# A different order of the expert units: two pairs behind the fixed experts, then every trio, then the last pair

## What is computed

```python
h = h + mixer(rms_norm(h, norm_mix[i]))
h = h + hier_moe(rms_norm(h, norm_ffn[i]), ...)      # the part that is reordered
h = h + sigmoid(rms_norm(h, ple_norm[i]) @ w_gate + b_gate) * (p[i] @ w_proj)

def hier_moe(m):            # every token goes to 2 of 32 experts of one group
    experts, weights = two_best_experts(m)
    for each expert e, for each block of 128 of its tokens:
        hb = silu(xb @ w_gate[e]) * (xb @ w_up[e])   # 1024 -> 512
        yb = hb @ w_down[e]                          # 512 -> 1024
    return sum over the two experts of weight * yb
```

## Time and profile before

| what | us |
|---|---|
| median of three runs | 3104.18 (3093.74 to 3106.1) |
| the profiled execution, its own time | 3108.6 |
| its span from first to last instruction | 3107.1 |
| units of layer 0's mixture, first to last product | 834.5 to 1386.9 |
| units of layer 1's mixture, first to last product | 2374.1 to 2929.1 |

### The profile page before, as it was taken

The page is one execution under the profiler, slowest core; times in us unless marked ns, Lnnn a source line. Parts: engine busy times, 40 slices in busy tenths (PEclk is TensorE's granted clock), DMA queues, the critical chain, the costliest instruction groups (busy, mean ns, idle before and its releaser), DMA issues. The chain is left out here.

```text
span 3107.1 us, 40774 instructions
## 1 busy us (share of the span) xinstructions
PE 2821.6 (91%) x16517; PEld 1453.9 (47%) x16518; DVE 1113.7 (36%) x2450; ACT 650.5 (21%) x1254; POOL 251.2 (8%) x376
## 2 busy tenths in 40 slices
PE   7999999999899898889989999877998988889898
PEld 4544555555533232224477744477655322223343
DVE  2585355544300000005463635566563000000152
ACT  3310355531110000004321123322211000000130
POOL 0000000001100000001000000144201000000110
PEclk9999999999899999989999899988998999999899
DMA  4000691031799999975020110000418999999731
GB/s 159 28 28 0 280 408 71 1 118 55 275 342 393 394 395 392 396 316 210 34 66 1 18 67 28 0 2 29 158 55 314 356 394 400 396 391 399 299 138 41
DMA packets 137045, 609.37 MB, mean 196 GB/s; under 512 B 25700, under 2 KB 32260, under 8 KB 120456
## 3 DMA queue, kind: packets, MB, share of 16 engines
q1 hardware_dynamic: 111848, 529.08, 44.4%
q0 software_dynamic: 21632, 74.46, 6.6%
q10 hardware_dynamic: 3376, 3.19, 0.3%
HBM read 503.80 MB, written 101.71 MB: 195 GB/s over the span
## 5 line engine op out<-in xcount | busy, mean ns | idle before, releaser
L1984 PE MATMUL acc<-wg,xt 128*128 128x512 f32 x512 | 224.5, 599 | 0.0
L1703 PE MATMUL py<-place 128*32 128x512 f32 (+2 forms) x816 | 154.8, 617 | 18.0 <-issue 17.4
L2638 PE MATMUL acc<-xt,work 128*128 128x512 f32 x384 | 166.9, 593 | 0.0
L672 PE MATMUL acc<-h,xt 128*128 128x512 f32 x384 | 165.2, 592 | 0.0
L1984 PEld LDWEIGHTS acc<-wg,xt 128*128 128x128 f32 x512 | 98.2, 193 | 120.8 <-issue 120.8
L310 PE MATMUL scores<-qkt 65*128 65x512 f32 (+7 forms) x384 | 146.0, 489 | 0.4 <-DVE qkt L451 0.4
L1703 PE MATMUL pg<-place 128*32 128x512 f32 (+2 forms) x640 | 123.2, 594 | 0.1
L457 DVE TENSOR_REDUCE nmax<-scores 128x1 f32<-128x256 f32 (+7 forms) x128 | 96.8, 757 | 73.9 <-PE scores L312 70.7
L1703 PE MATMUL pu<-place 128*32 128x512 f32 (+2 forms) x528 | 119.9, 612 | 0.1
L672 PEld LDWEIGHTS acc<-h,xt 128*128 128x128 f32 x384 | 72.9, 190 | 91.1 <-issue 90.9
L1214 PE MATMUL acc<-place 128*128 128x512 f32 x256 | 112.7, 594 | 1.1 <-PEq L71 1.1
(11 more groups left out here) (646 smaller groups left out, 5353.1 us busy)
## 6 DMA issues: line engine op xcount, KB each, us to landing
place<-in_moe_w_down_dram SPq DMA_DIRECT2D x23, 2048.0 KB, 28.2
own<-in_moe_w_up_dram SPq DMA_DIRECT2D x20, 2048.0 KB, 26.3
slots_out<-zeros SPq DMA_DIRECT2D x4, 9216.0 KB, 63.0
own<-in_moe_w_gate_dram SPq DMA_DIRECT2D x18, 2048.0 KB, 23.6
place<-in_moe_w_gate_dram SPq DMA_DIRECT2D x18, 2048.0 KB, 24.6
place<-in_moe_w_up_dram SPq DMA_DIRECT2D x17, 2048.0 KB, 26.1
own<-in_moe_w_down_dram SPq DMA_DIRECT2D x16, 2048.0 KB, 25.5
xt<-in_moe_w_down_dram SPq DMA_DIRECT2D x9, 2048.0 KB, 29.9
```

Source lines behind the costliest of these rows:

```text
L672: last = pe.matmul(acc[:, n % 4, 0:width], xs[:, k, tile_of(i)], weights[:, k, cols], start=(k == 0), stop=(k == k_of - 1))
L1703: last = pe.matmul(out[part], lhs[:, k, part], weights_of(kind, q)[:, k, cols], start=(k == 0), stop=(k == k_last), skip_group_check=True)
L1984: last = pe.matmul(acc[:, u % 4, :], xt[:, k, i * P:(i + 1) * P], wg[:, k, n * SLAB:(n + 1) * SLAB], start=(k == 0), stop=(k == KD - 1))
L2638: last = pe.matmul(acc[:, n % 4, :], slabs[m // 4 % 2][:, k, (m % 4) * P:(m % 4 + 1) * P], xt[:, k, half * SLAB:(half + 1) * SLAB], start= ...
```

## The change

Only `expert_units` is edited. It makes the same units with the same number of rows, in another sequence: units 0 and 1 are the fixed experts as before, units 2 and 3 are now pairs, units 4 to 19 the eight trios, unit 20 the last pair. The light experts are handed out from the front of one list, so the two early pairs now have the four most loaded light experts; the light expert of a trio stands four places further down the load in the first three trios, two in the next three, and is the same in the last two. `weight_order`, `mixer_end`, `preloads` and `first_blocks` call `expert_units` and follow.

```diff
 def expert_units():
     heavies, lights = list(range(FIXED, HEAVY)), list(range(HEAVY, EXPERTS))
     ranks, units = list(range(FIXED)), [[Part(q, 0, P)] for q in range(FIXED)]
     trios, pairs = len(heavies) // 2, (len(lights) - len(heavies) // 2) // 2
     assert 2 * trios == len(heavies) and trios + 2 * pairs == len(lights)
+
+    def pair():
+        q = len(ranks)
+        ranks.extend([lights.pop(0), lights.pop(0)])
+        units.append([Part(q, 0, 2 * QUAD), Part(q + 1, 2 * QUAD, 2 * QUAD)])
+
+    for n in range(pairs - 1):
+        pair()
     for n in range(trios):
         q = len(ranks)
         ranks += [heavies.pop(0), heavies.pop(0), lights.pop(0)]
         units += [[Part(q, 0, 3 * QUAD), Part(q + 2, 3 * QUAD, QUAD)],
                   [Part(q + 1, 0, 3 * QUAD), Part(q + 2, 3 * QUAD, QUAD, QUAD)]]
-        if pairs * (n + 1) // trios > pairs * n // trios:
-            q = len(ranks)
-            ranks += [lights.pop(0), lights.pop(0)]
-            units.append([Part(q, 0, 2 * QUAD), Part(q + 1, 2 * QUAD, 2 * QUAD)])
+    pair()
     return ranks, units
```

## The result

The changed kernel takes 3087.18 us (median of 14 runs, 3079.26 to 3092.93). Beside it the kernel before took 3101.88 (14 runs, 3093.27 to 3112.39). The ratio is 0.995, with a 95% interval of 0.9938 to 0.9962: 12 to 19 us faster, 15 in the middle. That is inside the predicted range of 3084 to 3108 and at the edge of what the prediction called no change (0.5%), but nearly twice the sum of 8.6 us on record and with its middle above the forecast's own gain of 4 to 12 us. One later execution of the changed kernel took 5421 us at a granted clock of 0.816 and is left out of every number here. The profiled execution took 3090.64 us with a span of 3089.1 us, where that of before had a span of 3107.1.

The account below looks back on a forecast made before the run. DMA was taken to bound both expert stages, with room only at their starts. The median of 3104.2 us less 8.6 (4.0 in layer 0, 4.6 in layer 1), middle at nothing, gave 3095.6 us; range 3084 to 3108.

Parts of the forecast that it names:

- the sum of 8.6 us on record: Both layers' expert stages: predicted gain from filling DMA at the start, 4.0 us in layer 0 plus 4.6 in layer 1.
- the forecast's own gain of 4 to 12 us: Whole kernel: likeliest case, only the start gains, giving 3092 to 3100 us; chance 0.70.
- What bounds it: Expert stages: DMA is full at 396 GB/s, PE waits for it, stage ends some 9 us after its last byte.
- Start: Stage start, 22.5 us: early pairs free two places per product, so DMA is full from 888.5, not 911; 8.6 us together.
- the two ends given: Bounds on the start's gain in both layers together: 4.0 us from below by share, 11.8 us from above by landings.
- Middle: Around the old middle pairs: PE waits of 13.3 and 12.0 us go away but are costed at nothing, DMA being full.
- The lower bound by share: Stage start: gain by DMA share alone, which counts a slow packet as busy; 1.8 plus 2.2, 4.0 us together.
- PE's first wait: Layer 0: at unit 4's up, needing matrix 21, ending near 937 us instead of 981.49.
- End: Stage end: same last three pieces, so last landing and products move forward by DMA's saving, landing near 1374, 4 us sooner.
- The idle time: Rival, trios: SP's list runs short later and one trio per layer loses the start's 4.3 us; 3104.2 us, chance 0.17.
- PE's waits at the old pairs: Rival, middle: PE sets the pace, so 13.3 + 12.0 us per layer go with the pairs; 3053.6 us, chance 0.07.
- PE's clock: Rival, trios: restarts at the low clock after waits make PE the bound, losing 37 us; 3133 us, chance 0.06.

Follow-up runs that it names:

- the 4 KB packets: Gate and up loaded as two DMAs of every other 4 KB, in both orders: order of before 3106.72 us, changed order 3096.77 us.
- TTTTTTTTPPP: Behind the fixed experts eight trios (T), then three pairs (P), against the order of before: first 3098.86 us, ratio 0.9988; 6.2 us gained over both passes.

## Why the prediction was right, and where it was short

**What bounds it: right.** DMA is full, PE waits for it, and the stage ends some 9 us behind its last byte, as it did.

**Start: right, and so was its size.** By the same method, bytes in 22.5 us, it gained 22.5 x (395 - 326)/396 = 3.9 us in layer 0 and, at the same place of the stage, 22.5 x (395 - 315)/396 = 4.5 in layer 1, 8.5 together where 8.6 stood. By landings it is 30.0 - 24.7 = 5.3 us per layer, 10.6 in all, between the two ends given. By times, 9.3 us for one pair in front (which takes one pair out of the middle as well), and 10 us with the 4 KB packets. The loads went out in twos, as said.

**Middle: this step failed.** "I cost that at nothing: DMA is full through them, and the bytes still have to come." The bytes came, but a full DMA isn't one rate: share counts a slowed packet as busy, and the 16 KB packets took 640 ns on average before and 628 after. Without pairs between the trios 459.7 - 455.8 = 3.9 us per layer fall away, 6.2 us in all by the times of the order that has this half alone (in its profiled stages the way from the last landing to the last product is 1.1 us per layer shorter too, so not all of that need be the middle's). That the time fell inside the stated range all the same was luck: the range had 8 us added below the forecast's 3092 for the spread of a median, and the middle's gain used them. The lower bound by share named the effect ("counts a slow packet as busy") for the start, and the middle was not held against it. That the rate can differ was to be seen: 405 GB/s at 1.01 about one pair, 394 at 1.01 about the other, 395 at 1.02 for trios; the share was nearly the same, the rate not. Which way it would go these short stretches didn't say (there the pairs look the faster, if anything), but even 1% over 449 us is 4.5 us per layer, either way, and it stood nowhere in the sum.

**PE's first wait: sooner than said.** It was due near 937, at up of unit 4, and came at 926, at down of unit 3, ending at 929.76. That product needs the down matrices 18 and 19. By 5.90 us per matrix from number 13 on they were due at 918.9 and 924.8, before it. They were issued at 903.49, and the view of DMA's issues has, as the mean of the two from issue to landing:

```profile
place<-in_moe_w_down_dram SPq DMA_DIRECT2D x2, 2048.0 KB, 23.4
```

So 926.9 in the middle of the two and not 921.9; by their landings, 924.6 and 929.7. The mean of 5.90 us spreads a unit's rows evenly, but they come in lumps: 0.99 MB of them moved between the landings of 17 (915.8) and 18. No cost of this wait is seen: DMA was full behind it.

**End: right, in layer 0 by chance.** The last matrix of layer 0 was to land near 1374 and its products started at 1373.95. But this was the stage of the changed order with the most slow packets (991) and the longest rest (458.0 us); in the two other executions it landed at 1370.2 and 1366.7. Layer 1's stage, due to end at 2920.5, ended at 2912.3, by the middle's gain and the scatter of single executions (it began 4.6 us sooner).

**The rivals.** The idle time did not return: share is 1.01 to 1.02 in every row of the changed kernel shown behind the start. PE's waits at the old pairs were not the price: they are gone in TTTTTTTTPPP too, which gained 6 us and not 50. PE's clock did not decide: it was granted 0.95 and 0.97 in the two stages, 0.96 and 0.95 before, and PE's waits for matrices, up to 3.6 us each in layer 0 (4.2 before), did not make PE the bound: DMA's share stayed full.

**What stays open.** Why fewer large packets meet rows where the trios are unbroken. It differs from one execution to the next (in the three profiled ones of the changed order a stage had 122 to 991 slow packets), so it isn't fixed by the order alone. That two pairs between the trios do more harm than one is shown by the landings of four stages each, not by the times; that it is the break in the rhythm of rows and loads is only argued. The experiment with 4 KB packets takes away the gain together with the large packets, but it also doubles the loads, and it has one profiled execution for each order. The sizes are uncertain too: the profiled stages alone would give TTTTTTTTPPP 12 us and one pair in front 16, more than their times do; both profiled executions of before (3108.6 and 3105.9) lie above before's medians, so the times were taken.

## What to carry to other kernels

Where a stage is bound by its bytes, look for the stretch in which the queue isn't fed: put first the work that frees buffers fastest, and last the work with the least left to do behind its last byte. A busy share of 1.0 doesn't say that the rate is the best: compare GB/s between stretches of full share, and hold their spread against every step that is costed at nothing because the queue is full. When a gain comes out larger than its sum, run each half of the change alone.

## What the runs showed of the hardware

At full share, over layer 0's 449 us, DMA moved 394 to 401 GB/s. The size of the weights' packets, 4 or 16 KB, hardly changed that rate: from the page's part on queues, layer 0's rest (queue, packets, MB, share of 16 engines over 449 us) of before and then with 4 KB packets alone:

```profile
q1 hardware_dynamic: 20658, 160.55, 90.2%
```

```profile
q1 hardware_dynamic: 41064, 159.87, 91.3%
```

Twice the packets carry the same bytes in nearly the same share. Of the 41,064 some 2,000 have 4 bytes and take 9 ns; the 39,028 of 4 KB take 168 ns on average, so four take 670 ns, against 635 on average for one of 16 KB in the same stretch of before. The rate was 394 GB/s, where 396 were had with the large packets; the 28 to 38 us that I had expected of the small ones were 4. Two things went the other way: 4 KB packets took 178 ns among the large ones and 168 among their like, and the share over all queues rose from 1.02 to 1.03, that is, more packets overlapped. The large ones, 617 ns with no rows in flight, took 657 to 727 with some. The Trainium skill, page "DMA: Bandwidth & Descriptors", section "Queues, rings and completion order", says that a DMA engine takes turns between its queues packet by packet, where a packet is as a rule a group of descriptors; the trace agrees so far as a large packet gets longer while those of another queue are in flight, while it shows neither in which steps they took turns nor whether a packet of the profile is one of that page.
